# The small projection of a three-branch layer: tokens on the output partitions instead of features

## The chip, the core and the metric

The kernel runs on one core of one Trainium2 chip. The metric is device time in microseconds, as the median of several executions. TensorE is called PE below (PEld is its weight-load row), VectorE DVE, ScalarE ACT, GpSimd POOL, SyncE SP.

## The reference, cut to what matters

Two blocks follow one another, each of two layers, on 512 tokens of width 1024. The edit is in the first block. Its layer normalises x and multiplies it by one wide matrix, whose columns are split over three branches:

```python
proj = h @ w_in[l]                       # [512, 1024] @ [1024, N_IN]
(gq, gk, gv, ga, gz, bq, bk, bv, iq, ik, iw, bz,
 cq, ck, cv, cz, gate) = jnp.split(proj, SPLIT_AT, axis=-1)
# gated linear attention: ga [T, 16] gives the decay rates
log_a = log_sigmoid(ga @ gla_wa2[l] + gla_ba[l]) / 16
# indexer of the sparse attention: ik [T, 64], iw [T, 8]
dots  = einsum('bqhd,bsd->bqhs', iq, ik) * 64 ** -0.5
score = einsum('bqhs,bqh->bqs', relu(dots), iw * 8 ** -0.5)   # then top-128 of it
```

Three narrow groups of columns, ga (16), ik (64) and iw (8), are computed together as the unit "small": 88 columns.

## The kernel before, in words

All engines walk one list of steps, `line`, that `make_timeline` writes by hand; each engine takes from a step what is its own, and semaphores order them. A projection is a *unit*: it is cut into quarters of 256 rows of the weight, and into slices, each of which fills one PSUM bank. A *sweep* step is two slices by one quarter on PE. Each product is made of three fp32r passes (high x high, high x low, low x high), so a sweep of a 512-wide unit has 2 slices x 2 chunks x 3 passes = 12 matmuls. A slice of mode `tok` has a tile of 128 tokens as the stationary operand and the weight's columns as the moving one; its output has tokens on the partitions. Mode `feat` has the weight's columns stationary and tokens moving; `feat0` and `feat1` take 256 tokens each.

Each weight piece is loaded by SP into a ring of six slots, ACT copies it to fp32r (`high`, line 1070), POOL subtracts to get the low part (line 693). `high(g)` waits until piece g - 5 has been used (`SPLIT = 5`) and is called on ACT ahead of the copies of the sweep's outputs (`evacuate`).

The unit small is special: one quarter with all eight chunks of 128 rows, so one piece of 704 columns. It has two slices, `feat0` and `feat1`, and so one sweep. Its output has features on the partitions: ik on 0 to 63, iw on 64 to 71, ga on 72 to 87. ACT copies ik to `ikT` (line 1113) and the other 24 rows to `gaT` (line 1114); DVE copies ik once more into `ikT`'s upper half (line 1411), because heads come in pairs on two halves of the partitions. `small_turn` transposes the 8 rows of iw for the four tiles on PE (line 813) and ACT scales them into `iwtok` (line 1206). The row of ones for `gla_ba` is a memset of `gaT` (line 1409).

Behind small come, in `line`: a modulation step in layer 0 (`mod`, for the second block, line 1813), `rstd bq`, `small_turn`, and then 32 `index` steps woven with bk's eight sweeps, four index products before each sweep (line 822 on PE, a relu on ACT at line 1212, a multiply-add on DVE at 1668 and 1671). bv's sweeps follow with the key transposes; then 48 top-k rounds on DVE (lines 1680 and 1682) beside gqk and gv on PE, the mask (line 1687), and the decay products `decay1` (line 829), which read `gaT` and `wab`. `mod` steps are spread evenly over a list of certain sweeps, of which small is one. PE's short products take their PSUM banks in turn from the ring `aux` of three banks, and wait until the bank's last user was read.

Of the kernel before, what the change touches and what calls it, by code (L numbers as in the profile page):

```python
# [16 lines left out]
ACT = mybir.ActivationFunctionType  # L17
# [6 lines left out]
P = 128  # L24
DEPTH = 2
# [67 lines left out]
def make_timeline(blocks=(1, 2), layers=DEPTH):  # L93
# [30 lines left out]
    if 1 in blocks:  # L124
        for l in range(layers):
# [3 lines left out]
            line.extend(U("iq", C_IQ, 512, feat()))  # L129
            line.extend(U("small", C_IK, 88, [("feat0", 0, 0, 88), ("feat1", 0, 0, 88)]))  # L130
            line.append(("rstd", l, "bq"))
            line.append(("small_turn", l))
            idx = [[("index", l, t, h)] for t in range(TILES) for h in range(IDX_HEADS)]
# [192 lines left out]
def build(nc, a, out, known=None, blocks=(1, 2), layers=DEPTH):  # L326
# [57 lines left out]
    with ExitStack() as ctx:  # L384
        def sb(name, shape, dt=F32):
            return ctx.enter_context(nc.sbuf_tensor(name, shape, dt))
# [48 lines left out]
        colT = sb("colT", [P, N_COLS])  # L435
        wab = sb("wab", [P, 256])
        glag = sb("glag", [P, DEPTH, P])
# [35 lines left out]
        iqT, ikT = region(32, 4, T), region(29, T)  # L473
        iwtok, gaT = region(24, 4, 8), region(27, T)
        rates = slice(64, 89)
        score = region(40, AT[-1] + WIDTH[-1])
# [38 lines left out]
        def piece(buffer, slot, u):  # L515

            v = buffer[:, slot].rearrange("p c n -> p (c n)")
            return v.rearrange("p (c n) -> p c n", c=u["chunks"])[:, :, 0:u["n"]]
# [25 lines left out]
        def _(sp):  # L544

            def load_weights(g):
                u, q = stream[g]
                if g >= RING:
                    sp.wait_ge(product, at("used", g - RING))
                slot = g % RING  # L550
                src = w_src[u["w"]](u)[u["row0"] + 256 * q:u["row0"] + 256 * q + P * u["chunks"], :]
                src = src.rearrange("(c p) n -> p c n", p=P)
                if u["name"] == "small":
                    sp.dma_start(piece(raw, slot, u)[:, :, 72:88], src[:, :, C_GA:C_GA + 16]).then_inc(raw_loaded[slot], mark(raw_loaded[slot], by=16))
                    sp.dma_start(piece(raw, slot, u)[:, :, 0:72], src[:, :, C_IK:C_IK + 72])\
                        .then_inc(raw_loaded[slot], mark(raw_loaded[slot], ("raw", g), by=16))
                elif u["name"][:3] == "mix" and q >= 2:
                    heads = w_src[u["w"]](u)[512:1024, u["col"]:u["col"] + u["n"]].rearrange("(g n d) c -> g d n c", g=2, d=64)
                    for g2 in range(2):
                        sp.dma_start(raw[64 * g2:64 * g2 + 64, slot, :, 0:u["n"]], heads[g2, :, 2 * q - 4:2 * q - 2])\  # L560
                            .then_inc(raw_loaded[slot], mark(raw_loaded[slot], *([("raw", g)] if g2 else []), by=16))
                else:
                    sp.dma_start(raw[:, slot, :, 0:u["n"]], src[:, :, u["col"]:u["col"] + u["n"]])\
                        .then_inc(raw_loaded[slot], mark(raw_loaded[slot], ("raw", g), by=16))
# [35 lines left out]
            for step in line:  # L600
# [29 lines left out]
                elif step[0] == "vectors":  # L630
                    l = step[1]
                    if l > 0:
                        sp.wait_ge(product, at("rates", l - 1, TILES - 1))
                    sp.dma_start(wab[rates], a["rate_rows"][l]).then_inc(rates_loaded, mark(rates_loaded, ("wab", l), by=16))
                elif step[0] == "mod":
# [63 lines left out]
        def _(pe):  # L699
# [20 lines left out]
            def sweep(i, p, q):  # L720
# [10 lines left out]
                for k, (mode, idx, c0, n) in enumerate(pair):  # L731
# [20 lines left out]
                    for c in range(u["chunks"]):  # L752
                        x = 2 * q + c
                        for n_pass, (A, W, ring) in enumerate(((Ah, wh, SPLIT), (Ah, wl, RING), (Al, wh, SPLIT))):
                            w = piece(W, g % ring, u)[:, c]
                            if mode == "tok":
                                args = (o[:, 0:n], A[:, x, idx * P:(idx + 1) * P], w[:, c0:c0 + n])
                            elif mode == "feat":
                                args = (o, w[:, c0:c0 + n], A[:, x, :])
                            else:  # L760
                                lo = 256 * int(mode[4])
                                args = (o[0:n, 0:256], w[:, c0:c0 + n], A[:, x, lo:lo + 256])
                            last = pe.matmul(*args, start=(q == 0 and c == 0 and n_pass == 0),  # L763
                                             stop=(q == u["quarters"] - 1 and c == u["chunks"] - 1 and n_pass == 2))
# [13 lines left out]
            for step in line:  # L778
# [29 lines left out]
                elif kind == "small_turn":  # L808
                    _, l = step
                    b = bank("aux", step)  # L810
                    pe.wait_ge(act_result, at("small", l, 1))
                    for t in range(TILES):
                        last = pe.transpose(b[:, 8 * t:8 * t + 8], gaT[64:72, t * P:(t + 1) * P], ident[64:72, 64:72])
                    last.then_inc(product, mark(product, ("turned", step)))
                elif kind == "index":
                    _, l, t, h = step
                    b = bank("aux", step)
                    half = slice(64 * (h % 2), 64 * (h % 2) + 64)
                    for half_t in range(t // 2 + 1):
                        pe.wait_ge(dve_result, at("keys", l, half_t))  # L820
                    pe.wait_ge(act_result, at("iq", l, h // 2))
                    pe.matmul(b[:, 0:WIDTH[t]], iqT[half, h // 2, t * P:(t + 1) * P], ikT[half, 0:WIDTH[t]],
                              start=True, stop=True).then_inc(product, mark(product, ("dots", step)))
                elif kind == "decay1":
                    _, l, t = step
                    b = bank("aux", step)
                    pe.wait_ge(act_result, at("small", l, t // 2))
                    pe.wait_ge(rates_loaded, at("wab", l))
                    pe.matmul(b[:, 0:256], gaT[rates, t * P:(t + 1) * P], wab[rates], start=True, stop=True)\
                        .then_inc(product, mark(product, ("rates", l, t)))  # L830
# [231 lines left out]
        def _(act):  # L1062
# [19 lines left out]
            def evacuate(i, s):  # L1082
# [28 lines left out]
                elif name == "small":  # L1111
                    act.wait_ge(dve_result, at("ones_row", l))
                    act.activation(ikT[0:64, 256 * s:256 * s + 256], b[0:64, 0:256], ACT.Copy)
                    act.activation(gaT[64:88, 256 * s:256 * s + 256], b[64:88, 0:256], ACT.Copy)\
                        .then_inc(act_result, mark(act_result, ("small", l, s)))
                elif name == "gqk":
# [46 lines left out]
            for step in line:  # L1163
# [39 lines left out]
                elif kind == "small_turn":  # L1203
                    _, l = step
                    act.wait_ge(product, at("turned", step))
                    act.activation(iwtok, ps[:, bank_of.get(step, 0), 0:32].rearrange("p (t h) -> p t h", t=TILES), ACT.Copy,
                                   scale=float(np.float32(IDX_HEADS ** -0.5) * np.float32(0.125)))\
                        .then_inc(act_result, mark(act_result, ("small_turned", l), ("free", step)))
                elif kind == "index":
# [169 lines left out]
        def _(dve):  # L1379
# [20 lines left out]
            def evacuate(i, s):  # L1400
# [5 lines left out]
                key = ("scr", i, s)  # L1406
                if name == "small":
                    if s == 0:
                        dve.memset(gaT[64:96, :], 1.0).then_inc(dve_result, mark(dve_result, ("ones_row", l)))
                    dve.wait_ge(act_result, at("small", l, s))  # L1410
                    dve.tensor_copy(ikT[64:128, 256 * s:256 * s + 256], b[0:64, 0:256])\
                        .then_inc(dve_result, mark(dve_result, ("keys", l, s), free))
                elif name in ("ek", "eq"):
                    nh = 4 if name == "ek" else 8
# [113 lines left out]
            for step in line:  # L1528
# [100 lines left out]
                elif kind == "rstd":  # L1629
# [5 lines left out]
                    if name[0] == "e":  # L1635
                        nh = {"ek": 4, "eq": 8}[name]
                        s, v = stat[:, SS[name], 0:4 * nh], nsm[:, 0, 0:4 * nh]
                        dve.tensor_scalar(v, s, 1.0 / 64, EPS, ALU.mult, ALU.add).then_inc(dve_result, mark(dve_result))
                        dve.wait_ge(dve_result, now(dve_result))
                        rsqrt(s, v)  # L1640
                        continue
                    dve.tensor_scalar(v, s, nh / 512.0, EPS, ALU.mult, ALU.add).then_inc(dve_result, mark(dve_result))
                    dve.wait_ge(dve_result, now(dve_result))
# [15 lines left out]
                elif kind == "index":  # L1659
# [5 lines left out]
                    s = score[:, AT[t]:AT[t] + W]  # L1665
                    w = iwtok[:, t, h:h + 1]
                    if h == 0:
# [334 lines left out]

INPUTS = ["x", "norm_g", "w_in", "gla_norm_g", "dsa_qn_g", "dsa_kn_g", "diff_qn_g", "diff_kn_g",
          "diff_lq1", "diff_lk1", "diff_lq2", "diff_lk2", "w_br", "w_out", "c_2", "w_mod_2", "b_mod_2", "norm1_2",
# [65 lines left out]
```

## Time and profile before

| what | value |
|---|---|
| median of 3 runs | 2840.59 us (2836.87 to 2846.26) |
| the profiled execution's own time | 2836.87 us |
| its span, first to last instruction | 2834.8 us |
| mean granted TensorE clock | 0.955 |
| PE matmuls busy | 2523.5 us, 89% |
| DVE, ACT, POOL busy | 51%, 33%, 31% |

A matmul's record is longer than the distance to the next start, because matmuls are pipelined: pace is read from starts, not from durations. Granted clock 1.00 is the 2.4 GHz level and 0.50 the 1.2 GHz level.

### The profile page before, as it was taken

The numbers are of one execution on the slowest core, as the hardware profiler recorded it, in microseconds if no ns is written. First come the engines' busy times: TensorE is split into PE (matmuls) and PEld (weight loads), VectorE is DVE, ScalarE is ACT, GpSimd is POOL, SyncE is SP. The second block draws the span as 40 slices with busy tenths as digits, with TensorE's granted clock in tenths as the row PEclk, the third lists the DMA queues.
The fourth block names the chain that finished last, engine by engine and source line by source line (L and its number), as shares of the span: only waits on it lengthen the run. The fifth ranks groups of instructions, "written<-read, shape, count | busy, mean of one in ns | idle before, by whom it ended". The sixth has DMA issues, their size and how long they took to land. (4 is left out here: it accounts for less than half of the span.)

```text
span 2834.8 us, 34357 instructions
## 1 busy us (share of the span) xinstructions
PE 2523.5 (89%) x12303; PEld 2008.5 (71%) x12303; DVE 1439.2 (51%) x2993; ACT 943.5 (33%) x1695; POOL 878.7 (31%) x366
## 2 busy tenths in 40 slices
PE   5998999889999899989977878999997777899999
PEld 4676877677768677767776547878776644787877
DVE  4496243654368733365465456454556554623334
ACT  3433243432343224342233442322223354232221
POOL 2332314233324242323422002454442200244442
PEclk9999999999999999999998799999998889999999
DMA  4232414134323241313432002444433200233332
GB/s 140 88 90 67 148 39 134 45 97 164 126 65 90 90 141 54 110 58 106 162 88 64 1 1 60 141 162 142 147 121 83 64 1 1 60 95 99 95 96 77
DMA packets 133573, 256.01 MB, mean 90 GB/s; under 512 B 23382, under 2 KB 30116, under 8 KB 133412
## 3 DMA queue, kind: packets, MB, share of 16 engines
q1 hardware_dynamic: 133412, 253.83, 28.5%
q8 instruction: 105, 1.72, 0.2%
q14 instruction: 56, 0.46, 0.1%
HBM read 249.60 MB, written 4.19 MB: 90 GB/s over the span
## 5 line engine op out<-in xcount | busy, mean ns | idle before, releaser
L693 POOL TENSOR_TENSOR wl<-raw,wh 128x1024 fp32r<-128x1024 f32 (+2 forms) x362 | 878.5, 2431 | 1928.5 <-ACT wh L1070 1927.3
L763 PE MATMUL ps<-wh,hTh 128*128 128x512 f32 (+3 forms) x1600 | 645.6, 403 | 16.1 <-DVE hTl L1626 16.1
L1070 ACT ACTIVATE wh<-raw 128x1024 fp32r<-128x1024 f32 (+2 forms) x362 | 379.9, 1049 | 841.4 <-PE ps L763 440.9
L763 PE MATMUL ps<-wl,hTh 128*128 128x512 f32 (+3 forms) x1600 | 625.7, 391 | 0.0
L763 PE MATMUL ps<-wh,hTl 128*128 128x512 f32 (+3 forms) x1600 | 625.2, 391 | 0.0
L763 PEld LDWEIGHTS ps<-wh,hTh 128*128 128x128 f32 x1600 | 311.9, 195 | 86.2 <-issue 30.8
L763 PEld LDWEIGHTS ps<-wh,hTl 128*128 128x128 f32 x1600 | 310.6, 194 | 60.3
L763 PEld LDWEIGHTS ps<-wl,hTh 128*128 128x128 f32 x1600 | 312.1, 195 | 52.7
L763 PE MATMUL ps<-hTh,wh 128*128 128x512 f32 (+2 forms) x704 | 258.8, 368 | 4.9 <-DVE hTl L1626 3.7
L763 PE MATMUL ps<-hTh,wl 128*128 128x512 f32 (+2 forms) x704 | 257.8, 366 | 0.0
L763 PE MATMUL ps<-hTl,wh 128*128 128x512 f32 (+2 forms) x704 | 257.7, 366 | 0.0
L717 PE MATMUL ps<-cf,arena 128*128 128x128 f32 x800 | 133.5, 300 | 136.2 <-DVE arena L1982 23.7
L717 PEld LDWEIGHTS ps<-cf,arena 128*128 128x128 f32 x800 | 101.8, 154 | 175.9 <-issue 82.7
L1813 DVE SCALAR_TENSOR_TENSOR modw<-modw,cact 128x1024 f32<-128x1024 f32 x96 | 151.2, 1581 | 139.9 <-DMA modw<-in_w_mod_dram 139.1
L763 PE MATMUL ps<-wh,yTh 128*128 128x512 f32 x448 | 178.7, 399 | 9.9 <-DVE scr L1450 9.9
L763 PE MATMUL ps<-wl,yTh 128*128 128x512 f32 x448 | 176.0, 393 | 0.0
L763 PE MATMUL ps<-wh,yTl 128*128 128x512 f32 x448 | 175.7, 392 | 0.0
L763 PEld LDWEIGHTS ps<-hTh,wh 128*128 128x128 f32 (+1 forms) x704 | 132.7, 189 | 27.3 <-issue 6.1
L763 PEld LDWEIGHTS ps<-hTh,wl 128*128 128x128 f32 (+1 forms) x704 | 132.7, 189 | 21.3
L763 PEld LDWEIGHTS ps<-hTl,wh 128*128 128x128 f32 (+1 forms) x704 | 132.7, 188 | 21.3
L1448 DVE TENSOR_SCALAR scr<-ps 128x512 f32<-128x512 f32 (+1 forms) x72 | 45.1, 627 | 180.2 <-PE ps L763 180.2
L1463 DVE TENSOR_TENSOR arena<-ps,arena 128x512 f32<-128x512 f32 x96 | 66.3, 691 | 109.3 <-PE ps L763 108.3
(262 smaller groups left out, 3277.1 us busy)
## 6 DMA issues: line engine op xcount, KB each, us to landing
raw<-in_w_in_dram SPq DMA_DIRECT2D x160, 512.0 KB, 3.6
raw<-in_w_ff_dram SPq DMA_DIRECT2D x128, 512.0 KB, 3.7
modw<-in_w_mod_dram SPq DMA_DIRECT2D x96, 512.0 KB, 4.7
raw<-in_w_br_dram SPq DMA_DIRECT2D x24, 512.0 KB, 3.7
raw<-in_w_out_dram SPq DMA_DIRECT2D x24, 512.0 KB, 3.7
xm<-in_x_dram SPq DMA_DIRECT2D x8, 512.0 KB, 4.5
raw<-in_w_out_dram SPq DMA_DIRECT2D x16, 256.0 KB, 3.9
raw<-in_w_in_dram SPq DMA_DIRECT2D x8, 408.0 KB, 3.3
```

Of the source, the lines that this page charges most:

```text
L693: pool.tensor_tensor(piece(wl, g % RING, u), piece(raw, g % RING, u), piece(wh, g % SPLIT, u).bitcast(F32), ALU.subtract)\
L717: last = pe.transpose(dst[:, c * P:(c + 1) * P], src[:, c * P:(c + 1) * P], ident)
L763: last = pe.matmul(*args, start=(q == 0 and c == 0 and n_pass == 0), stop=(q == u["quarters"] - 1 and c == u["chunks"] - 1 and n_pass == 2))
L1070: act.activation(piece(wh, g % SPLIT, u), piece(raw, g % RING, u), ACT.Copy)\
L1448: dve.tensor_scalar(tmp, b, 0.0, None, ALU.max).then_inc(dve_result, mark(dve_result))
L1463: dve.tensor_tensor(acc, b, acc, ALU.add).then_inc(dve_result, mark(dve_result, free))
L1813: dve.scalar_tensor_tensor(w, w, 0.5, cact[:], ALU.mult, ALU.mult, accum_out=modT[:, m // MOD_STEPS, m % MOD_STEPS:m % MOD_STEPS + 1])\
```

## The change

The unit small becomes token-major. It has four `tok` slices of 88 columns and so two sweeps; the columns come in the order ga, ik, iw. ACT's evacuation writes a tile's ik twice side by side, ga, and the scaled iw into one token-major buffer `smtok`. `small_turn` is now a step for each tile: PE transposes the doubled ik (128 columns) and ga (16 columns), and ACT copies them to `ikT` and `gaT`. DVE has no copy for this unit; the memset of the ones row moves into the step `rstd bq` and covers 32 rows from partition 0. The decay product has 17 rows instead of 25, and `wab` comes straight from two inputs in two DMAs.

```diff
-            line.extend(U("small", C_IK, 88, [("feat0", 0, 0, 88), ("feat1", 0, 0, 88)]))
+            line.extend(U("small", C_GA, 88, tok(88)))
             line.append(("rstd", l, "bq"))
-            line.append(("small_turn", l))
+            line.extend([("small_turn", l, t) for t in range(TILES)])
...
-        iwtok, gaT = region(24, 4, 8), region(27, T)
-        rates = slice(64, 89)
+        smtok, gaT = region(24, 4, 152), region(27, T)
...
-                    sp.dma_start(wab[rates], a["rate_rows"][l]).then_inc(rates_loaded, mark(rates_loaded, ("wab", l), by=16))
+                    sp.dma_start(wab[0:16], a["gla_wa2"][l]).then_inc(rates_loaded, mark(rates_loaded, by=16))
+                    sp.dma_start(wab[16:17], a["gla_ba"][l:l + 1, :]).then_inc(rates_loaded, mark(rates_loaded, ("wab", l), by=16))
...
                 elif kind == "small_turn":
-                    _, l = step
+                    _, l, t = step
                     b = bank("aux", step)
-                    pe.wait_ge(act_result, at("small", l, 1))
-                    for t in range(TILES):
-                        last = pe.transpose(b[:, 8 * t:8 * t + 8], gaT[64:72, t * P:(t + 1) * P], ident[64:72, 64:72])
-                    last.then_inc(product, mark(product, ("turned", step)))
+                    pe.wait_ge(act_result, at("small", l, t))
+                    pe.transpose(b[:, 0:P], smtok[:, t, 0:P], ident)
+                    pe.transpose(b[0:16, P:2 * P], smtok[:, t, P:P + 16], ident)\
+                        .then_inc(product, mark(product, ("turned", step)))
                 elif kind == "index":
...
-                    for half_t in range(t // 2 + 1):
-                        pe.wait_ge(dve_result, at("keys", l, half_t))
+                    for tt in range(t + 1):
+                        pe.wait_ge(act_result, at("small_turned", l, tt))
...
-                    pe.matmul(b[:, 0:256], gaT[rates, t * P:(t + 1) * P], wab[rates], start=True, stop=True)\
+                    pe.matmul(b[:, 0:256], gaT[0:17, t * P:(t + 1) * P], wab[:], start=True, stop=True)\
...
                 elif name == "small":
-                    act.wait_ge(dve_result, at("ones_row", l))
-                    act.activation(ikT[0:64, 256 * s:256 * s + 256], b[0:64, 0:256], ACT.Copy)
-                    act.activation(gaT[64:88, 256 * s:256 * s + 256], b[64:88, 0:256], ACT.Copy)\
-                        .then_inc(act_result, mark(act_result, ("small", l, s)))
+                    act.activation(smtok[:, idx, 0:P].rearrange("p (r d) -> p r d", r=2),
+                                   b[:, 16:80].unsqueeze(1).to_broadcast([P, 2, 64]), ACT.Copy)
+                    act.activation(smtok[:, idx, P:P + 16], b[:, 0:16], ACT.Copy)
+                    act.activation(smtok[:, idx, P + 16:P + 24], b[:, 80:88], ACT.Copy,
+                                   scale=float(np.float32(IDX_HEADS ** -0.5) * np.float32(0.125)))\
+                        .then_inc(act_result, mark(act_result, ("small", l, idx), free))
...
                 elif kind == "small_turn":
-                    _, l = step
+                    _, l, t = step
+                    b = ps[:, bank_of.get(step, 0)]
                     act.wait_ge(product, at("turned", step))
-                    act.activation(iwtok, ps[:, bank_of.get(step, 0), 0:32].rearrange("p (t h) -> p t h", t=TILES), ACT.Copy,
-                                   scale=float(np.float32(IDX_HEADS ** -0.5) * np.float32(0.125)))\
-                        .then_inc(act_result, mark(act_result, ("small_turned", l), ("free", step)))
+                    act.wait_ge(dve_result, at("ones_row", l))
+                    act.activation(ikT[:, t * P:(t + 1) * P], b[:, 0:P], ACT.Copy)
+                    act.activation(gaT[0:16, t * P:(t + 1) * P], b[0:16, P:2 * P], ACT.Copy)\
+                        .then_inc(act_result, mark(act_result, ("small_turned", l, t), ("free", step)))
...
-                if name == "small":
-                    if s == 0:
-                        dve.memset(gaT[64:96, :], 1.0).then_inc(dve_result, mark(dve_result, ("ones_row", l)))
-                    dve.wait_ge(act_result, at("small", l, s))
-                    dve.tensor_copy(ikT[64:128, 256 * s:256 * s + 256], b[0:64, 0:256])\
-                        .then_inc(dve_result, mark(dve_result, ("keys", l, s), free))
-                elif name in ("ek", "eq"):
+                if name in ("ek", "eq"):
...
+                    if name == "bq":
+                        dve.memset(gaT[0:32, :], 1.0).then_inc(dve_result, mark(dve_result, ("ones_row", l)))
+                        dve.wait_ge(dve_result, now(dve_result))
```

## Rows read from the trace of the kernel before

**Rows 1.** The page: busy us of each engine, share of the span, instructions.
```profile
PE 2523.5 (89%) x12303; PEld 2008.5 (71%) x12303; DVE 1439.2 (51%) x2993; ACT 943.5 (33%) x1695; POOL 878.7 (31%) x366
```

**Rows 2.** Windows: stretch, its length, busy us and instructions of each engine, granted clock.
```profile
core 0: us, PE busy (x) PEld busy (x) DVE busy (x) ACT busy (x) POOL busy (x), PEclk, DMA share, GB/s
86.69:92.30 5.61, 5.61 (x49) 5.54 (x47) 0.00 (x0) 2.03 (x3) 4.49 (x2) 1.00 0.42 128
97.54:100.95 3.41, 3.41 (x9) 2.66 (x9) 2.92 (x15) 0.00 (x0) 0.00 (x0) 0.50 0.00 0
173.00:205.00 32.00, 32.00 (x188) 28.47 (x187) 30.42 (x69) 9.32 (x14) 12.16 (x5) 1.00 0.27 84
788.20:797.30 9.10, 6.36 (x24) 4.89 (x23) 4.98 (x20) 3.63 (x10) 2.34 (x1) 0.62 0.21 59
1503.10:1506.80 3.70, 3.70 (x40) 3.36 (x40) 0.69 (x1) 3.12 (x6) 3.68 (x2) 1.00 0.68 208
1551.60:1568.60 17.00, 12.22 (x66) 10.11 (x64) 8.31 (x34) 6.14 (x24) 1.28 (x1) 0.50 0.00 1
```

**Rows 3.** Timeline, layer 0, 74 to 97 us: start, length, engine, line, operation, idle time.
```profile
74.33 0.48 DVE L1409 MEMSET arena<- 32x512 f32 x1 [0.16 <-issue]
...
86.69 0.28 PE L763 MATMUL ps<-hTh,wh 128*88 128x256 f32 x1
...
88.79 1.06 ACT L1110 ACTIVATE arena<-ps 128x512 f32<-128x512 f32 x2
...
92.20 0.28 PE L763 MATMUL ps<-hTl,wh 128*88 128x256 f32 x1
...
92.57 1.06 ACT L1070 ACTIVATE wh<-raw 128x1024 fp32r<-128x1024 f32 x1 [2.72 <-PE ps L763]
...
93.53 0.36 ACT L1113 ACTIVATE arena<-ps 64x256 f32<-64x256 f32 x1
...
94.31 0.42 DVE L1411 COPY arena<-ps 64x256 f32<-64x256 f32 x1 [19.50 <-ACT arena L1114]
...
95.53 1.34 PE L822 MATMUL ps<-arena 64*128 64x128 f32 x8
...
96.80 0.50 PE L763 MATMUL ps<-wh,hTh 128*128 128x512 f32 x1
...
96.90 0.28 ACT L1212 ACTIVATE scr<-ps 128x128 f32<-128x128 f32 x1 [0.22 <-PE ps L822]
```

**Rows 4.** Timeline, layer 0, behind the index products: DVE's chain and PE's wait.
```profile
143.98 0.18 DVE L1397 SCALAR_TENSOR_TENSOR stat<-nsm,stat 128x16 f32<-128x16 f32 x1
...
209.09 2.18 DVE L1687 TENSOR_SCALAR maskb<-arena 128x512 bf16<-128x512 f32 x1
...
213.21 0.88 PE L829 MATMUL ps<-wab,arena 25*128 25x256 f32 x2 [2.44 <-DVE arena L1694]
```

**Rows 5.** Groups by form, PE and PEld: stationary shape, moving shape, count, busy, mean ns.
```profile
L763 PEld LDWEIGHTS ps<-hTh,wh 128*128 128x128 f32 x672 | 127.8, 190 | 27.2 <-issue 6.1
L763 PEld LDWEIGHTS ps<-hTh,wh 128*88 128x88 f32 x32 | 4.9, 154 | 0.1
L998 PE MATMUL ps<-arena 64*128 64x32 f32 x128 | 17.2, 275 | 0.0
```

**Rows 6.** Timeline, short products: start of a run of equal ones, its length, count.
```profile
209.21 1.56 PE L829 MATMUL ps<-wab,arena 25*128 25x256 f32 x6
...
1503.11 1.08 PE L932 MATMUL ps<-yarena 128*64 128x62 f32 x15
...
1548.85 1.07 PE L998 MATMUL ps<-arena 64*128 64x32 f32 x8
```

**Rows 7.** One line, the scaled copy of iw: count, shortest, median and longest ns, first and last start.
```profile
L1206 ACT ACTIVATE arena<-ps x2: 198/198/198, 95.6 to 791.8; 128x32 f32<-128x32 f32 x2
```

**Rows 8.** The tile wab: who writes and reads it, shortest, median, longest ns.
```profile
L829 PE MATMUL ps<-wab,arena x16: 374/374/557, 209.2 to 908.7; 25*128 25x256 f32 x16
L634 SPq DMA_DIRECT2D wab<-in_rate_rows_dram x2: 372/372/372, 64.1 to 760.0; - x2
```

More of the change, by code:

```diff
@@ L435, in build @@
         colT = sb("colT", [P, N_COLS])
-        wab = sb("wab", [P, 256])
+        wab = sb("wab", [17, 256])
         glag = sb("glag", [P, DEPTH, P])
@@ L553, in load_weights @@
                 if u["name"] == "small":
-                    sp.dma_start(piece(raw, slot, u)[:, :, 72:88], src[:, :, C_GA:C_GA + 16]).then_inc(raw_loaded[slot], mark(raw_loaded[slot], by=16))
-                    sp.dma_start(piece(raw, slot, u)[:, :, 0:72], src[:, :, C_IK:C_IK + 72])\
+                    sp.dma_start(piece(raw, slot, u)[:, :, 0:16], src[:, :, C_GA:C_GA + 16]).then_inc(raw_loaded[slot], mark(raw_loaded[slot], by=16))
+                    sp.dma_start(piece(raw, slot, u)[:, :, 16:88], src[:, :, C_IK:C_IK + 72])\
                         .then_inc(raw_loaded[slot], mark(raw_loaded[slot], ("raw", g), by=16))
@@ L761, in sweep @@
                                 lo = 256 * int(mode[4])
-                                args = (o[0:n, 0:256], w[:, c0:c0 + n], A[:, x, lo:lo + 256])
+                                args = (o[:, 0:256], w[:, c0:c0 + n], A[:, x, lo:lo + 256])
                             last = pe.matmul(*args, start=(q == 0 and c == 0 and n_pass == 0),
@@ L826, in _ @@
                     b = bank("aux", step)
-                    pe.wait_ge(act_result, at("small", l, t // 2))
+                    pe.wait_ge(act_result, at("small_turned", l, t))
                     pe.wait_ge(rates_loaded, at("wab", l))
-                    pe.matmul(b[:, 0:256], gaT[rates, t * P:(t + 1) * P], wab[rates], start=True, stop=True)\
+                    pe.matmul(b[:, 0:256], gaT[0:17, t * P:(t + 1) * P], wab[:], start=True, stop=True)\
                         .then_inc(product, mark(product, ("rates", l, t)))
@@ L1665, in _ @@
                     s = score[:, AT[t]:AT[t] + W]
-                    w = iwtok[:, t, h:h + 1]
+                    w = smtok[:, t, P + 16 + h:P + 17 + h]
                     if h == 0:
@@ L2000, in build @@
     return L
-INPUTS = ["x", "norm_g", "w_in", "gla_norm_g", "dsa_qn_g", "dsa_kn_g", "diff_qn_g", "diff_kn_g",
+INPUTS = ["x", "norm_g", "w_in", "gla_wa2", "gla_ba", "gla_norm_g", "dsa_qn_g", "dsa_kn_g", "diff_qn_g", "diff_kn_g",
           "diff_lq1", "diff_lk1", "diff_lq2", "diff_lk2", "w_br", "w_out", "c_2", "w_mod_2", "b_mod_2", "norm1_2",
@@ L2064 @@
     arrays = {n: np.ascontiguousarray(inputs[n]) for n in INPUTS} | constants()
-    arrays["rate_rows"] = np.concatenate([np.zeros((DEPTH, 8, 256), np.float32), inputs["gla_wa2"], inputs["gla_ba"][:, None]], 1)
     arrays["w_mod_2"] = np.ascontiguousarray(inputs["w_mod_2"].transpose(0, 2, 1))
```

## The prediction

> **What bounds the kernel now.** I read the page first: TensorE's matmuls cover 89% of the span, the next engine 51% [rows 1]. That average hides the stages, so I then asked for windows around the edited unit. While the small projection runs, PE is busy the whole stretch (5.61 of 5.61 us); in the 32 us in which the next products run beside the top-k it is busy all 32; behind the small projection comes a hole and a stretch at half clock [rows 2]. The timeline shows the hole's chain: the last small matmul starts at 92.20; ACT then makes the high part of a later weight piece (1.06 us), because its `high` waits for the small piece to be used up; only then come ACT's two copies for each half from 93.53, the 8-row transposes, four index products at 95.53 and the next sweep at 96.80 [rows 3]. So in this stage the order on PE sets the pace, and ACT's queue decides the hole.
>
> Does a delay here reach the end? The index products stand between bk's sweeps on PE. DVE scales four keys and does 48 top-k rounds after the last of them, from 143.98 without a pause to the mask at 209.09 (2.18 us), and PE waits 2.44 us for the fourth decay product behind it [rows 4]. Both paths begin at the delayed point, so nothing absorbs a delay: one microsecond here is one at the end, in each of two layers.
>
> **The change part by part.**
>
> *The sweep.* Before, one sweep: 2 halves x 8 chunks x 3 passes = 48 matmuls, 88 stationary columns and 256 moving ones. Starts run from 86.69 to 92.20, so (92.20 - 86.69)/47 = 0.117 us each, 5.6 us [rows 3]. After, two sweeps: 4 tiles x 8 x 3 = 96 matmuls, 128 stationary columns (tokens) and 88 moving ones. The arithmetic per instruction falls to a third, the instructions and weight loads double. The trace has no fp32r matmul under 256 columns. What it has:
> - A 128-column load takes 190 ns, an 88-column one 154 [rows 5]: 40 columns cost 36 ns, so 128 cost some 115 ns beyond the fixed part. A 256-column stream (0.117 us) just hides that; an 88-column stream, about 0.117 x 88/256 = 0.04 us, doesn't.
> - The nearest row is the short product of L998: 128 stationary columns, 32 moving. Eight start within 1.07 us, the last lasting 0.275: (1.07 - 0.275)/7 = 0.114 us apart [rows 5, 6], although it streams next to nothing. That is the weight load's pace.
>
> I take 0.114: 96 x 0.114 = 10.9 us, +5.3 a layer. Lower bound: streaming alone, 96 x 0.04 = 3.9 us (-1.7). Upper bound: short rows run at plain fp32's rate. L829's six instructions of 256 columns start (1.56 - 0.374)/5 = 0.237 us apart, and eight calls gave 16 instructions, two to a product [rows 6, 8], so 88 columns would cost 0.474 x 88/256 = 0.163 us, 15.6 us in all (+10.0).
>
> The row shows loads every 0.114 us. The Trainium skill ("TensorE: Matmul & The Clock Gate", section LDWEIGHTS) says that a load takes columns / 1.2 ns, 107 ns here, whatever the rows: the same answer, 10.3 us. The same page's section "Back-to-back issue gap" gives N/2.4 + 2.5 ns, 39 ns here, and would make the sweep 3.8 us, cheaper than before; it warns that this leaves the load out. The L998 row speaks against using it here. It is a rival below.
>
> *The turn and its copies.* Before, from the last small matmul (92.20) to the next full sweep (96.80) is 4.6 us [rows 3]. After, tiles 0 and 1 are evacuated and, on PE, turned while the second sweep runs or just behind it, so they cost nothing. What hides them is ACT, idle then: iq's last copies end at 89.85 [rows 3], 7.6 us before the longer sweep's last matmul (92.2 + 5.3); uncovered they would be two tiles' copies more, 1.3 us. Behind the sweep, with E for its last matmul's start (92.20 before): ACT's weight copy still goes first, ending near E + 1.4. Then six copies for tiles 2 and 3. A 128-column copy costs 0.28 (the 128x128 relu); 16 and 8 columns I put at 0.19 and 0.17, beside 0.198 for 32 columns [rows 3, 7]: 2 x 0.64 = 1.3, to E + 2.7. Then four turns of two 128-column copies each, 0.56 a tile. Four `small_turn` steps use PE's three aux banks, so tile 3's transposes wait for ACT's copy of tile 0 (E + 3.3), and the index products then wait for tiles 1, 2 and 3 to free theirs (E + 3.8, 4.4, 4.9); the fourth waits for the first relu, E + 5.3. The next sweep: about E + 5.6 instead of E + 4.6. I take +0.9 a layer, bounds 0 (transposes and copies overlap better) and +2 (each of the eight new copies costs 0.28 in full).
>
> *Removed.* Two DVE copies (0.42 each), four 24-row and four 64-row ACT copies a run each (0.36 the first), the iw turn [rows 3, 7]. The DVE ones lay under ACT's; the ACT ones are in the 4.6 us already.
>
> *Costed at nothing.* The ones row moves on DVE from the small evacuation to the head of `rstd bq`; DVE no longer waits for ACT there (it sat 19.50 us [rows 3]), so the memset (0.48 us [rows 3]) runs under the sweep; uncovered it is those 0.48. `wab` comes in two DMAs from SP instead of one, 17 rows instead of 25: one more issue (0.37 us) on SP's queue, 145 us ahead of its reader (64.1 and 209.21 [rows 6, 8]); the weight and modulation loads queued behind it wait for `used` pieces anyway; uncovered it is 0.37. The 17-row decay products have the same columns. The modulation steps are spread over a list that is two sweeps longer: three of them before small move one sweep later, the rest stay. POOL's subtraction for the unit and its two weight DMAs are of the same size.
>
> *Clock.* After each hole the granted clock is half: 97.54 to 100.95 in layer 0 (0.50, the 1.2 GHz level), 0.62 as mean of 788.2 to 797.3 in layer 1 [rows 2]. The hole stays about as long, so I take 0, with one half-clock stretch of 3.41 us more or less: at half clock 3.41 us do the work of 1.7, so that is 1.7 us either way.
>
> **Sum.** 2 x (5.3 + 0.9) = +12.4 us. Against the profiled execution's own 2836.87 (span 2834.8 and 2.1 around it) that is 2849.3. That execution is the fastest of three, 3.7 us under their median 2840.59; a forecast for a median starts there: 2853.0. The three lie 9.4 us apart, so 0.3% (8.5 us) is about what can be told from no change.
>
> **The rivals.**
> 1. *The clock falls inside the longer sweep.* For: PE's array would stream only 0.04 of every 0.114 us, and at 1551.6 to 1568.6, where PE is busy 12.2 of 17 us with short products, the granted clock is 0.50; against: 15 products of 62 columns back to back (1503.1 to 1506.8) kept 1.00, and there they fill their time [rows 2, 6]. If the second half of each sweep runs at half clock, 48 x 0.114 = 5.5 us more a layer: +11, so 2864.
> 2. *Short fp32r rows lose their rate* (0.163 us). For: every fp32r row here has 256 columns or more, so nothing shows that the fast rate holds under it; plain fp32 does cost four times as much a column. Against: at 256 columns, 0.117 us a start [rows 3], the fast rate is whole, with no sign of a fall. 2 x (10.0 + 0.9) = +21.8: 2862.
> 3. *The weight load doesn't bind* and the 88 columns stream at 0.04 us. 2 x (-1.7 + 0.9) = -1.6: 2839, no change. This is the other side; it decides if starts in the new sweep lie under 0.06 us (96 x 0.06 = 5.7, the old sweep). Against it: L998. The page's gap formula by which the sweep would be 3.8 us is this case.
> 4. *The half-clock stretches behind the hole vanish*, because the transposes of tiles 0 and 1 fill its start. They cost 1.7 us in layer 0; in layer 1, 0.62 over 9.1 us with PE busy for 6.36 of them makes some 2.4; without them the forecast's 2853.0 becomes 2848.9, at the edge of what can be told. Against: the hole is no shorter.
>
> **How the numbers follow.** My forecast (sweep bound by loads) 0.60, its own range 2845 to 2860: pace 0.108 to 0.12 (-1.2 to +1.2), hole 0 to +2 a layer (-1.8 to +2.2), a half-clock stretch a layer each way (3.4), and the runs' spread. Rival 1: 0.14; rival 2: 0.12; rival 3: 0.09; rival 4: 0.05. The range 2844 to 2865 takes in rivals 1, 2 and 4 and leaves out rival 3 and the tails. Slower by over 0.3% (above 2849.1): 0.85 of the forecast's 0.60, all of rivals 1 and 2, little else: 0.79. Within: 0.18. Faster: 0.03, since no part has 8 us to give.
>
> **What would show it.** In the profile after: 192 matmuls of 128x88, three names, with starts 0.11 us apart (0.04: rival 3; 0.16 at full clock: rival 2; 0.22 with granted clock 0.50: rival 1); the small stage 10.9 us long; PE's wait for ACT's turned copies, the next full sweep 5.5 us after the last small matmul; DVE no longer idle 19.5 us; the mask and everything later shifted by 6 us in layer 0, 12 in layer 1. Wrong most easily: the pace, a sixth of which is 2 us a layer, and half-clock stretches that fall elsewhere once all is shifted.

## The result, and the profile after

The changed kernel takes 2868.67 us (median of 6, 2864.07 to 2878.76), the kernel before beside it 2839.45 (6 runs). The ratio is 1.01, interval 1.0074 to 1.0126: slower by 21 to 36 us. The forecast was slower, 2853.0 in a range of 2844 to 2865; the direction was right, the size outside the range. The profiled execution's span is 2860.8 us, 26.0 more than before; its own time is 2862.72.

The page of the profile again hides it. PE has 36 us more busy time and stays at 89% (compare [rows 1]):

```profile
span 2860.8 us, 34637 instructions
PE 2559.2 (89%) x12407; PEld 2036.8 (71%) x12407; DVE 1437.6 (50%) x2989; ACT 945.9 (33%) x1725; POOL 877.4 (31%) x366
```

Windows around the small sweeps, as in [rows 2]: layer 0 cut where the pace changes, at the first full sweep behind the hole and at the end of the half-clock stretch, then the sweep of layer 1. The column behind POOL's is the granted clock.

```profile
core 0: us, PE busy (x) PEld busy (x) DVE busy (x) ACT busy (x) POOL busy (x), PEclk, DMA share, GB/s
87.10:91.70 4.60, 4.60 (x43) 4.60 (x42) 1.76 (x1) 2.34 (x6) 3.94 (x2) 1.00 0.73 283
91.70:103.20 11.50, 11.50 (x56) 11.50 (x55) 4.50 (x17) 0.42 (x3) 0.48 (x1) 0.50 0.00 1
103.20:108.03 4.83, 4.13 (x18) 2.56 (x18) 0.64 (x2) 3.78 (x18) 2.35 (x1) 0.50 0.67 217
108.03:112.17 4.14, 4.14 (x11) 3.27 (x11) 0.71 (x3) 0.28 (x1) 0.00 (x0) 0.50 0.00 0
796.50:801.60 5.10, 5.10 (x48) 5.10 (x46) 5.01 (x4) 2.34 (x6) 3.49 (x2) 1.00 0.76 247
801.60:812.10 10.50, 10.50 (x52) 10.50 (x51) 3.12 (x14) 0.42 (x3) 0.81 (x1) 0.50 0.00 0
```

PE never pauses in the sweep, yet from 91.70 on its clock is at 1.2 GHz, and stays there for 20 us, through the sweep's larger part, the hole and four microseconds of bk. No other engine began anything between 90.83 and 93.19. The timeline at the edge and in the hole, in the columns of [rows 3]:

```profile
91.37 0.29 PE L763 MATMUL ps<-wh,hTh 128*128 128x88 f32 x1
91.48 0.29 PE L763 MATMUL ps<-wl,hTh 128*128 128x88 f32 x1
...
92.15 0.42 PE L763 MATMUL ps<-wh,hTl 128*128 128x88 f32 x1
92.36 0.42 PE L763 MATMUL ps<-wh,hTh 128*128 128x88 f32 x1
...
103.03 0.42 PE L763 MATMUL ps<-wh,hTl 128*128 128x88 f32 x1
...
105.06 0.45 PE L812 MATMUL ps<-cf,arena 128*128 128x128 f32 x1 [0.70 <-ACT arena L1115]
...
106.15 1.95 PE L822 MATMUL ps<-arena 64*128 64x128 f32 x8
...
107.36 0.29 DVE L1669 TENSOR_SCALAR arena<-scr,arena 128x128 f32<-128x128 f32 x1 [10.63 <-ACT scr L1216]
...
108.03 0.79 PE L763 MATMUL ps<-wh,hTh 128*128 128x512 f32 x1
```

Starts are 0.11 us apart at full clock and 0.21 at half: the load's pace and its double. From the first small matmul to the first full sweep it is 108.03 - 87.10 = 20.9 us, before 96.80 - 86.69 = 10.1 [rows 3]: +10.8. Layer 1 has the same picture (796.48 to 816.88 after, 782.66 to 793.56 before): +9.5. Together 20.3 of the span's 26.0. The last mask behind the top-k starts 12.2 us later in layer 0 (221.26 against 209.09) and 23.4 us later in layer 1 (929.95 against 906.57), where 6 and 12 were forecast. The other 5.7 us of the span lie outside the edited stage; more on them below.

### The profile page after: what moved, and what is told of

The parts are those of the page before. It is cut to its first block and busy times, and to the rows that moved or that the text cites. A ratio compares the mean times of both kernels' runs of the same rounds, so it can differ in the third digit from the quotient of the medians.

```text
span 2860.8 us, 34637 instructions
## 1 busy us (share of the span) xinstructions
PE 2559.2 (89%) x12407; PEld 2036.8 (71%) x12407; DVE 1437.6 (50%) x2989; ACT 945.9 (33%) x1725; POOL 877.4 (31%) x366
## 5 line engine op out<-in xcount | busy, mean ns | idle before, releaser
L763 PE MATMUL ps<-wh,hTh 128*128 128x512 f32 (+4 forms) x1664 | 668.5, 402 | 14.6 <-DVE hTl L1624 14.6
L763 PE MATMUL ps<-wl,hTh 128*128 128x512 f32 (+4 forms) x1664 | 649.7, 390 | 0.0
L763 PE MATMUL ps<-wh,hTl 128*128 128x512 f32 (+4 forms) x1664 | 649.2, 390 | 0.0
L763 PEld LDWEIGHTS ps<-wh,hTl 128*128 128x128 f32 x1664 | 328.1, 197 | 60.5
L763 PE MATMUL ps<-hTh,wh 128*128 128x512 f32 (+1 forms) x672 | 250.0, 372 | 6.3 <-DVE hTl L1624 5.1
L763 PE MATMUL ps<-hTh,wl 128*128 128x512 f32 (+1 forms) x672 | 248.9, 370 | 0.0
L763 PE MATMUL ps<-hTl,wh 128*128 128x512 f32 (+1 forms) x672 | 248.8, 370 | 0.0
L763 PEld LDWEIGHTS ps<-hTh,wh 128*128 128x128 f32 x672 | 127.8, 190 | 28.6 <-issue 7.4
L763 PEld LDWEIGHTS ps<-hTh,wl 128*128 128x128 f32 x672 | 127.9, 190 | 21.2
L763 PEld LDWEIGHTS ps<-hTl,wh 128*128 128x128 f32 x672 | 127.7, 190 | 21.3
```

## The experiments

Ratios are to the kernel before, run on the same chip beside each; medians of before were 2842.46 (e1 to e4), 2842.82 (e5 to e8) and 2843.86 (e9, e10).

**e1: the changed kernel again.** No edit.

> The changed kernel once more, as the reference for its variants on one chip. Theory A (the clock falls in the load-bound sweep): +26 to +30 us over the kernel before, small sweeps of about 16 us a layer with starts first 0.111 and then 0.213 us apart. Theory B (a chance of phases: the fall comes in some executions only): the sweep takes 10.7 us in at least one layer and the difference is under 20 us.

Measured: 2863.83 us, ratio 1.009 (1.0065 to 1.0115). The small products took 15.8 and 15.6 us, with half clock from 91.5 and from 798.1, 20.5 us each:

```profile
86.80:102.60 15.80, 15.80 (x97) 15.80 (x95) 6.29 (x17) 2.76 (x9) 4.51 (x2) 0.65 0.21 81
793.10:808.70 15.60, 15.60 (x97) 15.60 (x95) 8.13 (x17) 2.76 (x9) 4.40 (x2) 0.66 0.25 83
```

So the fall is no matter of luck: in both layers of both profiles it came some 5 us after the start. Theory B falls. The median difference of 21 us lies under the 26 to 30 that were expected; the interval (18 to 33 us) reaches over both.

**e2: 176 moving columns instead of 88.**

```diff
-                            if mode == "tok":
+                            if u["name"] == "small":
+                                args = (o[:, 0:2 * n].rearrange("p (r n) -> p r n", r=2), A[:, x, idx * P:(idx + 1) * P],
+                                        w[:, c0:c0 + n].unsqueeze(1).to_broadcast([P, 2, n]))
+                            elif mode == "tok":
```

> The small product's moving operand is read twice (176 columns instead of 88; the second copy lands beside the first and nobody reads it). Theory A: the weight load (0.111 us) still hides the stream (176 columns are about 0.073 us), the array streams twice as much, the granted clock stays 1.00 in the sweep, starts stay 0.111 apart, the sweep falls from 16 to 10.7 us a layer, and the kernel is 11 to 15 us faster than the changed one although it computes more: some +14 us over the kernel before. Theory C (the many weight loads themselves bring the clock down, whatever is streamed): 0.213 and the half clock stay, +28 us.

Measured: 2852.05 us, ratio 1.004 (1.0021 to 1.0059): with twice the streaming, 12 us faster than e1. Windows over small's matmuls in both layers, and between them over the hole of layer 0:

```profile
85.58:96.30 10.72, 10.72 (x98) 10.72 (x97) 6.29 (x17) 2.76 (x9) 4.23 (x2) 1.00 0.33 124
96.30:100.14 3.84, 2.61 (x19) 1.68 (x17) 0.33 (x2) 3.57 (x18) 2.35 (x1) 1.00 0.67 199
791.44:802.20 10.76, 10.76 (x98) 10.75 (x97) 7.99 (x17) 2.76 (x9) 4.50 (x2) 1.00 0.35 118
```

The same 96 loads, the same instructions and turns, and the clock holds 1.00 through them. This run decides between the theories: the loads are as many and as fast, only the streaming beside them is doubled, and the clock doesn't fall (theory A over C).

**e3: 264 moving columns.** As e2, with 3 in place of 2.

> The same with the operand read three times, 264 columns: the stream (0.110 us and 0.013 between) is now as long as the load. Theory A with the load as the limit: starts 0.12 us apart, 11.8 us a layer, full clock, within 2 us of the 176-column kernel. If instead the stream were the limit in all of them, 176 to 264 columns would cost 96 x 0.037 x 2 = 7 us.

Measured: 2851.33 us, ratio 1.0038 (1.0021 to 1.0055), the same as e2. The sweep's commonest group by form (busy time, then mean ns of one), in e2:

```profile
L766 PE MATMUL ps<-wh,hTh 128*128 128x176 f32 x64 | 17.6, 275 | 0.0
```

The same group in e3:

```profile
L766 PE MATMUL ps<-wh,hTh 128*128 128x264 f32 x64 | 18.1, 283 | 0.0
```

Two neighbouring starts in e3's timeline:

```profile
90.25 0.28 PE L766 MATMUL ps<-wl,hTh 128*128 128x264 f32 x1
90.37 0.28 PE L766 MATMUL ps<-wh,hTl 128*128 128x264 f32 x1
```

And the window over e3's sweep in layer 0:

```profile
87.59:99.20 11.61, 11.61 (x98) 11.60 (x97) 6.31 (x17) 2.76 (x9) 4.80 (x3) 1.00 0.30 112
```

The sweep is 11.6 us against 10.7 in e2. Three times the columns of 88 cost one microsecond: at 88 and at 176 the starts are 0.11 us apart, as the load of 128 fp32r columns sets them, and the stream comes free; at 264 they are 0.12 apart, and the stream begins to count.

**e4: the kernel before, its small sweep computed twice.**

```diff
-                    for c in range(u["chunks"]):
+                    for c in [c for _ in range(2 if u["name"] == "small" else 1) for c in range(u["chunks"])]:
```

> The kernel before with its small sweep computed twice over (96 matmuls of 256 columns, the second 48 write the same result again). Theory A: full clock, 5.6 us more a layer and nothing else: +11 us, all of it present at the end of the kernel. Theory D (a delay at this place grows later on, or is partly absorbed): clearly more or less than 11 us.

Measured: 2850.47 us, ratio 1.0032 (1.0016 to 1.0048), which is 5 to 14 us. In the profile the sweep is 11.28 us at full clock, 5.7 more than in [rows 2], and the span 2846.0 is 11.2 over that of before: two layers' worth. On the way the shift isn't constant: 6.5 us at layer 0's last mask, 12.3 at layer 1's (918.85 against 906.57), 15.1 at ACT's weight copy at 1204.70 (here 1219.81), 11.2 at the end. So the 11.2 of one execution is partly chance, and what stands is the interval: a delay at this place reaches the end, one to one as far as 5 to 14 us for 11.3 can tell. That speaks against theory D. The window over layer 0's sweep, and the start of its last mask (before: 209.09 [rows 4]):

```profile
87.42:98.70 11.28, 11.28 (x97) 11.16 (x95) 0.00 (x0) 2.03 (x3) 4.58 (x2) 1.00 0.21 66
...
215.54 0.57 DVE L1687 TENSOR_SCALAR maskb<-arena 128x512 bf16<-128x512 f32 x1
```

**e5: the two small sweeps apart.**

```diff
-            line.extend(U("iq", C_IQ, 512, feat()))
-            line.extend(U("small", C_GA, 88, tok(88)))
+            iq = U("iq", C_IQ, 512, feat())
+            small = U("small", C_GA, 88, tok(88))
+            line.extend(iq[0:4] + small[0:1] + iq[4:8] + small[1:2])
```

> The changed kernel with the same instructions, but its two small sweeps apart: iq's first four sweeps, small's first, iq's last four, small's second. Theory A (what brings the clock down is a long stretch that streams little): two stretches of 5.3 us instead of one of 10.7 leave much less time at half clock, so the small sweeps take 5.3 to 8 us each instead of 16 together; 5 to 12 us faster than the changed kernel, +10 to +18 us over the kernel before. Theory C (the weight loads as such): each small sweep still falls to 0.213 us after its first few us, and nothing is gained.

Measured: 2859.79 us, ratio 1.0054 (1.0031 to 1.0077). Windows over the four small sweeps:

```profile
76.60:83.60 7.00, 7.00 (x49) 6.99 (x48) 0.00 (x0) 1.02 (x4) 0.00 (x0) 0.74 0.00 0
96.10:102.20 6.10, 6.10 (x49) 6.10 (x47) 5.88 (x8) 2.04 (x3) 5.17 (x2) 0.85 0.41 121
785.10:790.80 5.70, 5.70 (x49) 5.68 (x48) 0.00 (x0) 1.02 (x4) 0.00 (x0) 0.92 0.00 0
803.00:809.40 6.40, 6.40 (x49) 6.40 (x47) 6.13 (x9) 2.03 (x3) 5.46 (x2) 0.81 0.57 188
```

Identical instructions, sweeps of 5.7 to 7.0 us: 25.2 us for the four instead of 32. The clock still fell in each, 3.3, 4.3, 4.8 and 4.0 us after its start, and what ran behind paid for the rest of the stretch. Each sweep falling after its first few us is also what theory C said, so this run doesn't tell A from C; e2 does. Against the kernel before, the ratio is +15 us (9 to 22), inside the expected +10 to +18. Against the changed kernel it is 10 us less by the ratios of e1 and e5, 4 less by the medians; with both intervals overlapping, that gain isn't shown in the time of the whole kernel.

**e6: the changed kernel with small ahead of iq.**

```diff
-            line.extend(U("iq", C_IQ, 512, feat()))
             line.extend(U("small", C_GA, 88, tok(88)))
+            iq = U("iq", C_IQ, 512, feat())
+            line.extend(iq[0:4])
             line.append(("rstd", l, "bq"))
             line.extend([("small_turn", l, t) for t in range(TILES)])
+            line.extend(iq[4:8])
```

> The changed kernel with small's two sweeps ahead of iq's eight and the turns in the middle of iq. Theory A: the hole of 5.0 us between small and bk closes (only iq's own copies stand before the first index product), but the low-streaming stretch of 10.7 us is whole and the clock falls in it as before, with iq's first matmuls paying the rest of the half-clock stretch: 5 to 10 us faster than the changed kernel. Rival (the hole is part of what lowers the clock): the sweep runs at full clock too and the gain is over 15 us.

Measured: 2870.43 us, ratio 1.0098 (1.0068 to 1.0128): no gain. Windows of layer 0: small's first and second sweep and the first iq sweep behind them:

```profile
61.20:68.00 6.80, 6.80 (x49) 6.80 (x47) 3.42 (x5) 3.32 (x8) 4.07 (x2) 0.75 0.55 176
69.70:80.00 10.30, 10.30 (x51) 10.30 (x49) 1.75 (x10) 0.93 (x2) 0.00 (x0) 0.50 0.00 0
80.00:85.10 5.10, 5.10 (x13) 4.04 (x14) 0.00 (x0) 1.67 (x7) 2.37 (x1) 0.50 0.64 207
```

Both halves of my expectation for the clock came true: it falls in the sweep, 3.4 us after the start (4.7 in layer 1), and iq pays the rest. So the rival, that the hole lowers the clock, falls: here PE ran without a pause from bq's sweeps into small's. But the hole did not close. It moved behind iq, where ACT's weight copy stands ahead of iq's own copies in the same way, and the timeline shows PE waiting 2.48 us for it, with a half-clock stretch of 6.8 us from then on. The expected 5 to 10 us were a miss.

```profile
109.15 0.79 PE L824 MATMUL ps<-arena 64*128 64x128 f32 x2 [2.48 <-ACT scr L1218]
```

**e7 and e8: the kernel before, mended at its hole.** In e7 ACT copies small's outputs before the weight copy that waits for small's piece; in e8 small goes ahead of iq as in e6.

```diff
+                    small = units[i]["name"] == "small"
+                    if small:
+                        evacuate(i, 2 * p)
+                        evacuate(i, 2 * p + 1)
                     while made[0] < min(unread[step] + SPLIT, G):
                         high(made[0])
                         made[0] += 1
-                    if q == units[i]["quarters"] - 1:
+                    if q == units[i]["quarters"] - 1 and not small:
```

> The kernel before, with ACT's copies of small's outputs ahead of the weight copy that waits for small's piece. The hole of 4.6 us loses most of the 1.06 us weight copy: 2 us less in two layers, perhaps one half-clock stretch less (1.7 us); if the hole's length were set elsewhere, no difference.

> The kernel before, with small's sweep ahead of iq's. The hole of 4.6 and 5.4 us and the half-clock stretches of 3.4 and 6.8 us behind it go: 3 to 4 us a layer and about 2 us of clock: 6 to 10 us faster than the kernel before. If the hole only moves (iq's last copies then stand before the index products), 0 to 3 us.

Measured: e7 2839.7 us, ratio 0.9984 (0.9966 to 1.0003), not told apart from no change, although its timeline shows the hole shorter, 91.36 to 94.38 = 3.0 us instead of 4.6, and the profile has no half-clock stretch behind the hole in either layer (before: 3.4 and 6.8 us). What may have taken this gain away is told at the end of the next section.

```profile
91.36 0.28 PE L763 MATMUL ps<-hTl,wh 128*88 128x256 f32 x1
...
91.68 0.38 ACT L1113 ACTIVATE arena<-ps 64x256 f32<-64x256 f32 x1 [1.64 <-PE ps L763]
...
94.38 0.50 PE L763 MATMUL ps<-wh,hTh 128*128 128x512 f32 x1
```

e8: 2835.68 us, ratio 0.9976 (0.9957 to 0.9996), faster by 1 to 12 us. The larger gain that was expected, 6 to 10 us, is neither shown nor excluded; as in e6, ACT's queue made a new wait of 2.41 us behind iq (e8's timeline):

```profile
92.99 1.06 ACT L1072 ACTIVATE wh<-raw 128x1024 fp32r<-128x1024 f32 x1 [1.48 <-DMA raw<-in_w_in_dram]
93.95 1.06 ACT L1112 ACTIVATE arena<-ps 128x512 f32<-128x512 f32 x2
94.91 0.61 ACT L1214 ACTIVATE scr<-ps 128x128 f32<-128x128 f32 x3
95.24 0.49 PE L824 MATMUL ps<-arena 64*128 64x128 f32 x2 [2.41 <-ACT scr L1214]
```

**e9: e8, with the early copies of e7 for small and for iq.**

```diff
+                    ahead = units[i]["name"] in ("small", "iq") and q == units[i]["quarters"] - 1
+                    if ahead:
+                        evacuate(i, 2 * p)
+                        evacuate(i, 2 * p + 1)
```

> The kernel before with small's sweep ahead of iq's, and ACT's copies of small's and iq's outputs ahead of the weight copy that waits for their pieces. The wait of 2.68 us that small-first left behind iq (ACT's weight copy at 92.99, then iq's copies, then the relus) should shrink to under 1.5 us and no half-clock stretch should follow it: 5 to 12 us faster than the kernel before. If the remaining gaps are absorbed or the clock falls elsewhere instead, within 4 us of it.

Measured: 2840.75 us, ratio 0.9977 (0.9957 to 0.9997): the same as e8. PE's wait fell only from 2.41 to 1.63 us, and a half-clock stretch of 3.4 us still came in layer 0 (the mean of the window below is 0.72). Of the expected 5 to 12 us the ratio's interval gives 1 to 12 with 6.5 in its middle, the medians 3: neither shown nor excluded, and no gain over e8.

```profile
92.25 0.48 PE L824 MATMUL ps<-arena 64*128 64x128 f32 x2 [1.63 <-ACT scr L1218]
...
90.40:96.40 6.00, 4.37 (x14) 3.27 (x13) 3.60 (x6) 2.06 (x6) 4.57 (x2) 0.72 0.53 175
```

**e10: e2 with ACT's copies ahead.** The edit of e7 on the kernel of e2.

> The changed kernel with 176 moving columns and ACT's copies ahead of the weight copy: the best token-major form tried. Theory A: full clock in the sweep (10.6 us) and a hole of 3 instead of 4 us, so 2 us less than the 176-column kernel: +7 to +11 us over the kernel before; the 5 us a layer that the longer, load-bound sweep costs can't be had back.

Measured: 2850.41 us, ratio 1.0012 (0.9994 to 1.003). The clock holds 1.00 in both layers' small products (10.73 us in layer 0), and the hole is 3.65 us (95.45 to 99.10) against 3.98 in e2, where 3 were expected. Of the expected +7 to +11 us the interval gives -2 to +9, the medians 6.6. The best token-major form tried is at most 0.3% over the kernel before; it isn't shown to beat it.

```profile
84.87:95.60 10.73, 10.73 (x98) 10.72 (x97) 6.30 (x17) 3.18 (x12) 4.18 (x2) 1.00 0.32 121
```

## Why the prediction was right and wrong

**The sweep's pace: right.** The forecast took 0.114 us from L998 and 10.9 us a layer. At full clock the starts are 0.111 apart and the sweep takes 10.7 us (e2). That weight loads bind is shown by e3, where three times the columns cost one microsecond. Rival 2, fp32r losing its rate on short rows, would be 0.163 us at full clock and is out; so is rival 3, streaming at 0.04 us. Only the first two starts (87.10, 87.14) are that close: the first load (86.88) ran under iq's last matmul. Rival 4, that the half-clock stretches behind the hole vanish, can't be read from the changed kernel, whose clock was already down; in e2 layer 0 kept its stretch (mean clock 0.57 from 100.14 to 104.10), layer 1 had none (1.00 from 806 to 815).

**Pass-through: right, as far as the spread can tell.** e4 put 5.7 us of full-clock work into the same place twice and got 5 to 14 by its interval, 11.2 in the profile. That nothing absorbs a delay rested on one chain in layer 0.

**The hole: taken too long, a small error.** I took +0.9 us a layer. In the changed kernel, at half clock, it is 5.0 us in both layers against 4.6 and 5.4 before: +0.4 and -0.4. At full clock (e2, layer 0) it is 3.98 us instead of 4.60, so -0.6. The mis-sized term is ACT's: I added up the records of the short copies (0.28, 0.19, 0.17), 1.3 us for six. Yet their starts are closer than the records are long, in e2:

```profile
97.49 0.26 ACT L1115 ACTIVATE arena<-ps 128x128 f32<-128x128 f32 x1
97.65 0.17 ACT L1117 ACTIVATE arena<-ps 128x16 f32<-128x16 f32 x1
97.71 0.18 ACT L1118 ACTIVATE arena<-ps 128x8 f32<-128x8 f32 x1
97.77 0.29 ACT L1115 ACTIVATE arena<-ps 128x128 f32<-128x128 f32 x1
```

Three copies take 97.77 - 97.49 = 0.28 us, not 0.64; the two copies of a turn come 0.31 us after those of the turn before, not 0.56. I had read PE's pace from starts and ACT's from durations.

**The clock: the step that failed.** "The hole stays about as long, so I take 0" costed the clock only behind the hole. The fall inside the sweep was rival 1, with a chance of 0.14. Its mechanism was right and its price about right: 5.5 us a layer were put for half of the sweep at half clock; measured are 16.1 us against 10.7 in layer 0 and 15.6 in layer 1, so 5.4 and 4.9. From first start to last start, small's matmuls take 15.9 and 15.4 us where they took 5.5 before: +10.4 and +9.9. The holes add +0.4 and -0.4, which makes the 20.3 us of the stage; e1's stage has 20.4. On the forecast's own base, 2840.59, that is 2860.9. So the clock alone doesn't bring the sum to the measured median of 2868.67: the 7.8 us above it are the rest below, which is only in part explained. What misled the chance: the row against the rival, L932's 62 columns at full clock, fills its time with streaming and says nothing of a stretch that streams a third of it (0.04 of 0.114 us, the prediction's estimate), as I noted there and then did not weigh; and nearness to rows of another kind (L998 comes sixteen at a time, within 2 us) had stood for a pace that must last 11 us. The Trainium skill ("TensorE: Matmul & The Clock Gate", section "Why this matters for your kernels") has a row on thin-M matmuls: loop so that all K-tiles (the blocks of the summed dimension) come before the next DMA, or pad M, else the clock oscillates. The row speaks of loops with DMA between the K-tiles; here PE paused for nothing in the sweep and the clock fell all the same, so the trace shows a case that the row doesn't cover. In its padding it is near e2, which widened the moving side, 88 columns read twice, and whose sweeps stayed at 1.00.

**The rest: in part a second wait, in part open.** 5.7 us of the profiled 26.0 lie outside the stage. From bk's first sweep to the first gate sweep the profiled execution lost 3.5 us in layer 0 and 1.4 in layer 1; e1's lost 0.7 and 6.2 in the same two parts, so this is not one fixed wait. One piece of it is behind the top-k, where PE waits for the last decay product. First layer 0 of the changed kernel:

```profile
221.14 2.34 POOL L693 TENSOR_TENSOR wl<-raw,wh 128x1024 fp32r<-128x1024 f32 x1 [0.30 <-ACT wh L1070]
221.26 2.50 DVE L1688 TENSOR_SCALAR maskb<-arena 128x512 bf16<-128x512 f32 x1
...
224.85 1.21 PE L829 MATMUL ps<-wab,arena 17*128 17x256 f32 x2 [4.17 <-DVE arena L1695]
```

Then the same place in e1, the same kernel:

```profile
219.25 0.51 DVE L1688 TENSOR_SCALAR maskb<-arena 128x512 bf16<-128x512 f32 x1
...
224.24 0.84 PE L829 MATMUL ps<-wab,arena 17*128 17x256 f32 x2 [2.25 <-DVE arena L1695]
```

The same mask takes 2.50 us where POOL's subtraction began just before it, and ends 0.3 us behind that one; where POOL stood still it takes 0.51. PE's wait is 4.2 us in the one and 2.3 in the other. In the twelve profiles, two layers each, the mask took 2.47 us or more ten times, with a wait of 4.1 to 4.3 us each time; in the other fourteen layers the wait was 2.2 to 2.5. The long wait stood in layer 0 of the changed kernel's profile and in layer 1 of e1's, the two parts that lost most; before had none. e7 had it in both layers, and the 1.7 us are about what its shorter hole saved in layer 0 (1.6). So some 1.7 us a layer hang on how POOL's work falls against the mask; how often each kernel meets the long wait is not known from one profile of each.

The remainder stays open. Half-clock stretches fall differently once all is shifted: by the mean granted clock (0.955 before, 0.947 after, 0.949 in e1) some 255, 303 and 292 us of the three executions ran at half clock, of which 10, 41 and 41 in the stage. e2 and e10, too, had more of them outside the stage than the kernel before, and e4 about as many. No run isolated them, and with medians whose intervals are 9 to 15 us wide they can't be told from the spread. The two medians of the changed kernel, 29 and 21 us over that of before, have the 20.3 of the stage just at their lower side.

## What to carry to other kernels

Turning this thin product, so that the wide side became stationary, doubled its weight loads, and with 128 stationary fp32r columns a matmul cost 0.111 us at full clock whether it streamed 88 columns or 176: count loads, not columns, while the moving side is as short as that. If such a stretch must last several microseconds, try giving it more to stream: useless columns that hide under the load were worth 12 us here. Read every engine's pace from the distance of starts, ACT's short copies too.

## What the runs showed of the hardware that was not expected

- PE that never paused fell to the 1.2 GHz level: ten times out of ten with matmuls of 88 columns every 0.111 us, 3.3 to 5.2 us after the first of them (both layers of the changed kernel, e1 and e6, and the four sweeps of e5). With 176 columns (e2, e10) or 264 (e3) it stayed at 2.4 GHz in all six layers.
- In e5 the four sweeps of 48 matmuls, 5.7 to 7.0 us each, had mean granted clocks of 0.74 to 0.92; none was at full clock throughout.
- Small ACT copies from PSUM overlap: 128 columns start 0.16 us before the next, 16 columns 0.06, with records of 0.26 and 0.17 us (e2).
- A DVE mask that takes 0.51 us alone took 2.50 us beside a POOL subtraction, and ended 0.3 us after it.
- At half clock the load-bound matmuls start 0.213 us apart instead of 0.111, so the loads hang on the granted clock; matmuls of 512 moving columns go from 0.23 us to 0.43.
